# Causal mask of the attention's diagonal blocks: accumulated by TensorE instead of added by VectorE

## What is computed

```python
def diff_attention(q, k, v, lam, subln_g, lambda_init):
    ...
    def block(args):                      # one block of 128 queries
        q_blk, i = args
        q_pos = i * Q_BLOCK + jnp.arange(Q_BLOCK)
        sc = jnp.einsum('bhcqd,bhckd->bhcqk', q_blk, kt).astype(jnp.float32)
        causal = k_pos[None, :] <= q_pos[:, None]
        sc = jnp.where(causal, sc, -jnp.inf)
        p = jax.nn.softmax(sc, axis=-1)
        p_diff = p[:, :, 0] - lam * p[:, :, 1]
        return jnp.einsum('bhqk,bhkv->bhqv', p_diff.astype(vt.dtype), vt)
    o = lax.map(block, (qb, jnp.arange(nb)))
    o = rms_norm(o, subln_g) * (1.0 - lambda_init)
```

## Time and profile before

| | us |
|---|---|
| median of 3 runs | 1903.6 (1900.66 to 1908.24) |
| the profiled execution | 1901.1 |
| its span, first to last instruction | 1899.3 |
| attention stage, about | 136 to 505 |
| TensorE busy in the span | 1839.1 (97%) |
| VectorE busy in the span | 1018.9 (54%) |
| mean granted clock of TensorE | 0.993 |

### The profile page before, as it was taken

The page is one execution under the profiler, slowest core; times in us unless marked ns, Lnnn a source line. Parts: engine busy times, 40 slices in busy tenths (PEclk is TensorE's granted clock), DMA queues, the critical chain, the costliest instruction groups (busy, mean ns, idle before and its releaser), DMA issues. The chain is left out here.

```text
span 1899.3 us, 25484 instructions
## 1 busy us (share of the span) xinstructions
PE 1839.1 (97%) x8808; PEld 1517.6 (80%) x8808; DVE 1018.9 (54%) x1594; ACT 637.1 (34%) x1243; POOL 195.4 (10%) x416
## 2 busy tenths in 40 slices
PE   6999999999999999999999999999999999999977
PEld 5877777777888888888888878788888888788866
DVE  4218888888612254332221455765555555577656
ACT  4216666666621132111122223333333333222111
POOL 2111121111110000000000012510000000000012
PEclk9999999999999999999999999999999999999989
DMA  6221111111161111111111422122212222322352
GB/s 214 89 56 34 57 57 56 56 56 45 56 252 47 40 55 50 51 45 56 44 45 55 133 88 91 65 92 80 91 70 88 83 85 75 111 92 96 99 188 89
DMA packets 129109, 153.41 MB, mean 81 GB/s; under 512 B 4800, under 2 KB 107712, under 8 KB 128016
## 3 DMA queue, kind: packets, MB, share of 16 engines
q1 hardware_dynamic: 114400, 97.27, 16.4%
q0 software_dynamic: 14352, 54.23, 7.9%
q10 hardware_dynamic: 288, 1.05, 0.2%
HBM read 120.02 MB, written 32.51 MB: 80 GB/s over the span
## 5 line engine op out<-in xcount | busy, mean ns | idle before, releaser
L1784 PE MATMUL ps<-xn,ring 128*128 128x512 f32 x1824 | 415.9, 389 | 0.0
L1784 PEld LDWEIGHTS ps<-xn,ring 128*128 128x128 f32 x1824 | 342.1, 188 | 71.3
L1784 PE MATMUL ps<-w_d,hn 128*128 128x512 f32 x1008 | 228.8, 389 | 0.0
L1188 DVE TENSOR_TENSOR ring<-raw,ring 128x1024 fp32r<-128x1024 f32 x76 | 96.5, 1269 | 245.8 <-ACT ring L677 245.6
L1784 PEld LDWEIGHTS ps<-w_d,hn 128*128 128x128 f32 x1008 | 189.2, 188 | 39.3
L1850 PE MATMUL ps<-xn,ring 128*128 128x512 f32 x864 | 214.2, 398 | 1.4 <-DVE qt L1261 1.0
L1850 PEld LDWEIGHTS ps<-xn,ring 128*128 128x128 f32 x864 | 158.3, 189 | 33.1 <-issue 1.1
L2051 PE MATMUL ps<-s_op,t_op_T 128*128 128x512 f32 x720 | 169.9, 389 | 0.0
L2051 PEld LDWEIGHTS ps<-s_op,t_op_T 128*128 128x128 f32 x720 | 135.2, 188 | 28.0
L677 ACT ACTIVATE ring<-raw 128x1024 fp32r<-128x1024 f32 x76 | 80.0, 1053 | 142.6 <-PE ps L1784 132.8
L1725 DVE TENSOR_TENSOR ff_sum<-ff_sum,ps 128x512 f32<-128x512 f32 x128 | 87.8, 686 | 52.6 <-PE ps L1784 52.6
(11 more groups left out here) (189 smaller groups left out, 2488.5 us busy)
## 6 DMA issues: line engine op xcount, KB each, us to landing
raw<-in_w_in_dram SPq DMA_DIRECT2D x58, 512.0 KB, 4.0
pair<-in_w_gate_up_dram SPq DMA_DIRECT2D x20, 1024.0 KB, 5.2
raw_down<-in_w_down_dram SPq DMA_DIRECT2D x22, 512.0 KB, 3.3
raw_down<-hf_scratch SPq DMA_DIRECT2D x22, 512.0 KB, 3.3
hf_scratch<-hf_out POOLq DMA_DIRECT2D x40, 256.0 KB, 2.3
y_scratch<-y_out POOLq DMA_DIRECT2D x8, 1024.0 KB, 4.2
ya<-y_scratch POOLq DMA_DIRECT2D x8, 1024.0 KB, 13.7
v_scratch<-v_out POOLq DMA_DIRECT2D x16, 256.0 KB, 2.4
```

The source lines that it names most:

```text
L1188: return dve.tensor_tensor(dst, src, hi.bitcast(F32), ALU.subtract)
L1784: last = pe.matmul(ps[:, bank, :], lhs, rhs, start=i == 0, stop=i == len(pairs) - 1)
```

## The change

The mask is no longer added by VectorE. `masked` is gone, and VectorE's `step_of` waits for the scores and goes straight to the maximum. Within TensorE's `scores`, after the first pass (two matmuls) of the chunk that holds the diagonal block, two matmuls of 128 columns are added, one for each component: a rounded identity as the stationary operand, a rounded mask as the moving one, accumulated into the diagonal block. GpSimd makes one mask of 128x128 instead of two; ScalarE rounds identity and mask to float32r once, ahead of the attention, and TensorE waits for that once.

```diff
@@ -196,7 +196,9 @@
         ident = const("ident", [P, P])
-        mask = const("mask", [P, 2, P])
+        mask = at("mask", [P, P], F32, RF + 31744)
+        ident_r = const("ident_r", [P, P], F32R)
+        mask_r = const("mask_r", [P, P], F32R)
@@ -240,6 +242,7 @@
+        mask_rounded = sem("mask_rounded")
@@ -507,11 +510,9 @@
-            for c in range(2):
-                did(pool.memset(mask[:, c, :], 0.0))
-                pool.affine_select(out=mask[:, c, :], in_=mask[:, c, :], compare_op=ALU.is_ge, fill=MASKED,
-                                   base=0, pattern=[[-1, P]], channel_multiplier=1).then_inc(mask_ready, 1)
-                pool.wait_ge(mask_ready, c + 1)
+            did(pool.memset(mask[:, :], 0.0))
+            pool.affine_select(out=mask[:, :], in_=mask[:, :], compare_op=ALU.is_ge, fill=MASKED,
+                               base=0, pattern=[[-1, P]], channel_multiplier=1).then_inc(mask_ready, 1)
@@ -866,6 +867,10 @@
             split_ring((proj_done, p.at()))
+            act.wait_ge(ident_ready, 1)
+            act.wait_ge(mask_ready, 1)
+            copy(ident_r[:, :], ident[:, :]).then_inc(mask_rounded, 1)
+            copy(mask_r[:, :], mask[:, :]).then_inc(mask_rounded, 1)
@@ -1280,12 +1285,6 @@
-            def masked(i):
-
-                dve.wait_ge(scores_done, t.at(1))
-                block = ps[:, i // 4:i // 4 + 3:2, P * (i % 4):P * (i % 4 + 1)]
-                did(dve.tensor_tensor(block, block, mask[:, :, :], ALU.add))
-
@@ -1309,7 +1308,7 @@
                 if not lag:
-                    masked(i)
+                    dve.wait_ge(scores_done, t.at(1))
                     maximum(i, 0)
                     maximum(i, 1)
@@ -1342,10 +1341,9 @@
-            dve.wait_ge(mask_ready, 2)
@@ -1866,6 +1864,10 @@
                                              start=n_pass == 0, stop=n_pass == 2)
+                        if n_pass == 0 and chunk == i // 4:
+                            for c in range(2):
+                                pe.matmul(ps[:, 2 * c + chunk, w - P:w], ident_r[:, :], mask_r[:, :],
+                                          start=False, stop=False, skip_group_check=True)
                 last.then_inc(scores_done, 1)
@@ -1927,6 +1929,7 @@
+            pe.wait_ge(mask_rounded, 2)
```

More of the change, by code:

```diff
@@ L1344, in _ @@
                 proj_lo_of(0, 1, half, first=True)
-            dve.wait_ge(mask_ready, 2)
             for i in range(TT):
                 step_of(0, i, first=True)
-            with turns(dve, (HEADS - 2) // 2, {n: 4, r: 4, p: 8, t: 16, trs: 40, step: 48, heads_in: 2}):
+            with turns(dve, (HEADS - 2) // 2, {n: 4, r: 4, p: 8, t: 16, trs: 40, step: 32, heads_in: 2}):
                 for par in (1, 0):
```

## The result

| | us |
|---|---|
| after, median (4 runs) | 1922.1 (1921.1 to 1925.6) |
| before, median (4 runs, on the same chip) | 1903.1 (1900.7 to 1908.2) |
| ratio | 1.0102, 95% interval 1.0087 to 1.0117 |
| after, profiled execution | 1921.1, span 1919.2 |

What follows compares the result with a forecast made beforehand. TensorE was taken to bound the attention stage, with VectorE second. Added mask matmuls, 35.8 us, less 17.5 us of stalls given back made +18.3: 1903.6 + 18.3 = 1921.9 us; forecast band 1912 to 1929, range 1901 to 1937.

Steps and rivals of the forecast that it cites:

- The bound: Attention stage: TensorE, busy 356.2 of 369 us, sets the time; VectorE, at 323.6, causes some 11 us of visible stall.
- The length of a head: Steady attention loop on TensorE: a head takes about 45.5 us before the change and 47.6 after.
- The mask pair: Two added 128-row matmuls amid TensorE's 64-row scores: 0.56 us a step, 35.8 us over 64 steps.
- The split: Within the added pair's 0.56 us: 0.22 to the first matmul, 0.12 to the second, 0.22 back to the scores.
- the rivals that priced the pair by the weighted values or by bare streaming: Cheaper prices for the added matmuls: 15.4 us in all (1901.5, chance 0.17) or 7.3 us (1893.4, chance 0.05).
- Rival 1: Added matmuls slip between the scores at the weighted values' pace: 15.4 - 17.5 = -2, 1901.5 us; chance 0.17.
- The stalls: TensorE's waits for VectorE at steps 5, 7 and 0: 2.4 us a head, 17.5 us taken as given back.
- the one point that had been called open: Second bank of transposes at step 0, waiting for `y_out`: a 0.5 us stall, its clearing within 0.2 us either way.
- VectorE's busy time: VectorE in the attention stage: some 28 us less busy, from 64 mask additions removed at 0.45 us each.
- The rest at nothing: ScalarE's two roundings, GpSimd's single mask and TensorE's wait for the rounding cost nothing; no DMA changes.

Runs made afterwards that it cites:

- the mask last: The changed kernel with its two mask matmuls behind the third pass, beside the transposes, instead of behind the first: 1905.9 us, ratio 1.0012.
- the two doses: The changed kernel with four 128-row mask matmuls instead of two: all behind the first pass, 1933.0 us; two behind each of the first two passes, 1954.2 us.
- the half rows: The changed kernel with each mask matmul cut into two of 64 rows, four in the same place: 1904.5 us, ratio 1.0002.

## Why the prediction was right, point by point

- **The bound.** TensorE was and is the bound of the stage, and what is late next is TensorE everywhere, as said: 1.9 us of its waits are left there, and 1.9 of its weight load's. The length of a head was misread: 45.5 us was the length of the window in the earlier trace rows. The scores of step 1 start at 323.94 in the earlier trace rows, and the same place a head later is 46.5 us on. After is at 48.8; the growth was forecast at 2.1 us a head and is 2.4, on a wrong base. The sum did not use it.
- **The mask pair.** 0.56 us a step was forecast from the gaps at both ends of a block of scores, 0.51 to 0.58 measured, 35 us against 35.8. The split was about right too: 0.23 to 0.28 for two matmuls and loads, the rest for the changes. The blocks of after rule out the rivals that priced the pair by the weighted values or by bare streaming. Rival 1's price for the matmuls, 0.24, is nearly what they cost beside the transposes (0.25 to 0.28); what it missed is the place, as the mask last, the two doses and the half rows show. What inside TensorE makes the gap at a change of rows, no run here takes apart. The rule of the Trainium skill, "TensorEngine Tiling (Array Packing)", Key Properties, is that a change of the tiling mode drains TensorE. All four of these kernels agree with it, with about 0.3 us for a way out and back in over the bare pair. The Trainium skill gives about 81 ns for each matmul in a stream of loads and 128-column matmuls ("TensorE: Matmul & The Clock Gate", Back-to-back issue gap). That does not hold here: it is 115 ns for each further 128-column matmul with its load.
- **The stalls.** 17.5 us given back was forecast; the traces say about 16 to 17 (10.8 in the transposes, 5.1 in the blocks, 0.9 in the rest), with 0.26 us a head left at the one point that had been called open, the second bank of step 0. The list of stalls was not exact: at step 5 of the last head there is none (five transposes in 0.52 us), and one of 0.57 at step 2 of the first head is missing. But the cause was only half right. The prediction asked whether VectorE's relief is given back whole, and counted TensorE's own delay as a help to it. Alone, the relief gives 10.6 to 12; alone, TensorE's delay gives 14 to 15. The sum came out because both were in it, and because the pair and the stalls were both taken a little too high. The change itself was +19.4 against +18.3 forecast; that the absolute forecast met the median within 0.2 us is luck.
- **VectorE's busy time** fell by 21.7 us, not 28. The 64 masks alone were 27 us, but in most steps the record of `y_out` in front still runs 0.08 us into the mask's (358.26 + 0.28 against 358.46), and the engine's total counts that time once. 64 times 0.42 - 0.08 is 21.8. Nothing else hangs on it.
- **The rest at nothing** held: TensorE's wait for the rounding shows in no list of waits, and the two roundings take 0.30 us each where ScalarE was idle.

## What to carry to other kernels

Moving work from a full engine to a fuller one is paid in full on the second and is worth, on the first, only the stalls that it ends. A stall that ends by the second engine coming later cannot be counted for both. Price an added matmul by where it stands: between 64-row matmuls a pair of 128 rows cost 0.3 us more here than beside other 128-row work, so put it where 128-row work already stands, or cut it to the rows of its neighbours. In a stage where two engines are nearly full, change the order of the helper's work one place at a time, and read after each which wait took over.

## What had not been expected of the hardware

- Four half-array matmuls with their loads (0.22 us) are cheaper in the middle of half-array work than two full ones (0.57 us), and a little cheaper than two full ones in the best place (0.25 to 0.28 us).
- At a change between 64-row and 128-row work, either way, the first weight load comes only with its matmul, where loads otherwise run ahead; behind 512-column scores the loads stand idle for 0.36 us with nothing to wait for. The price of a pair in the middle is nearly the same whatever stands in front: 0.51 us with 128-column scores, 0.56 with 256 columns, 0.57 with 512. A long matmul in front hides none of it.
